# Splitting a weight panel in two counted halves on VectorE

## What is computed

```python
def reference(...):
    x = first_block(x, c, positions, g_mix, w_ada, b_ada, w_in, ..., g_final)
    return second_block(x, c_2, ctx_2, c_ctx_2, ada_w_2, ada_b_2, ..., ffn_w_out_2)

# first_block, each layer (shortened)
    u = rms_norm(x, g_mix[l]) * (1 + sc_a) + sh_a
    proj = u @ w_in[l]
    ...
    x = x + gt_a * (merged @ w_out[l])
    u = rms_norm(x, g_ffn[l]) * (1 + sc_f) + sh_f
    h = jax.nn.silu(u @ w_ffn_gate[l]) * (u @ w_ffn_up[l])
    x = x + gt_f * (h @ w_ffn_down[l])
```

## Time and profile before

| | us |
|---|---|
| median of 3 runs | 2088.14 |
| lowest, highest | 2082.11, 2090.48 |
| the profiled execution | 2090.16 |
| its span, first to last instruction | 2088.3 |
| TensorE: matmuls under way | 2017.8 |
| TensorE: loading weights | 1827.4 |
| VectorE busy | 1624.2 |
| ScalarE busy | 1170.3 |
| GpSimd busy | 148.0 |

### The profile page before, as it was taken

The page is one execution under the profiler, slowest core; times in us unless marked ns, Lnnn a source line. Parts: engine busy times, 40 slices in busy tenths (PEclk is TensorE's granted clock), DMA queues, the critical chain, the costliest instruction groups (busy, mean ns, idle before and its releaser), DMA issues.

```text
span 2088.3 us, 37048 instructions
## 1 busy us (share of the span) xinstructions
PE 2017.8 (97%) x13975; PEld 1827.4 (88%) x13975; DVE 1624.2 (78%) x2668; ACT 1170.3 (56%) x2116; POOL 148.0 (7%) x233
## 2 busy tenths in 40 slices
PE   6999999999999999998999999999999999999998
PEld 6988999999988999997876888888887888998997
DVE  7888879966688879978687889786979436657983
ACT  6757756645557756646636455352544226656862
POOL 0100000100000000004000300001102000000000
PEclk9999999999999999999999999999999999999999
DMA  9866548765766557866341234546634223244553
GB/s 363 284 204 210 180 173 273 274 223 170 241 217 207 184 170 265 302 237 213 119 164 55 101 131 157 196 140 234 219 133 142 91 92 100 91 152 136 196 184 110
DMA packets 106624, 383.03 MB, mean 183 GB/s; under 512 B 11504, under 2 KB 16128, under 8 KB 105184
## 3 DMA queue, kind: packets, MB, share of 16 engines
q1 hardware_dynamic: 77584, 280.21, 39.3%
q0 software_dynamic: 25792, 94.31, 13.6%
q10 hardware_dynamic: 3088, 6.29, 0.9%
HBM read 379.71 MB, written 1.05 MB: 182 GB/s over the span
## 4 chain that ended last, share of the span: by engine, by line
PE 74%; DVE 13%; issue 4%; ACT 4%; DMA 3%; POOL 0%; POOLq 0%; DVEq 0%; SPq 0%; ACTq 0%
PE ps L1104 18%; PE ps L1108 17%; PE ps L1107 17%; DVE ring_l L2394 3%; DVE ada_junk L2417 3%; PE ps L1125 3%; PE ps L1129 3%; PE ps L1130 3%; PE ps L1147 2%; DMA work<-adas_in 2%; PE ps L1150 2%; PE ps L1151 2%; ACT ring_r L1734 2%; PE ps L1684 1%; DMA ring<-tape_in 1%
## 5 line engine op out<-in xcount | busy, mean ns | idle before, releaser
L1104 PE MATMUL ps<-part,ring_l 128*128 128x256 f32 (+1 forms) x3373 | 1012.4, 300 | 8.3 <-DVE ring_l L2394 8.1
L1108 PE MATMUL ps<-part,ring_r 128*128 128x256 f32 (+1 forms) x3373 | 1005.4, 298 | 0.0
L1107 PE MATMUL ps<-part,ring_r 128*128 128x256 f32 (+1 forms) x3373 | 1004.6, 298 | 0.0
L2394 DVE TENSOR_TENSOR ring_l<-ring,ring_r 128x1024 fp32r<-128x1024 f32 x514 | 626.6, 1232 | 142.8 <-ACT ring_r L1734 140.5
L1734 ACT ACTIVATE ring_r<-ring 128x1024 fp32r<-128x1024 f32 x514 | 533.6, 1056 | 332.4 <-DMA ring<-tape_in 235.6
L1104 PEld LDWEIGHTS ps<-part,ring_l 128*128 128x128 f32 x3373 | 635.2, 188 | 40.5 <-issue 8.8
L1107 PEld LDWEIGHTS ps<-part,ring_r 128*128 128x128 f32 x3373 | 635.4, 188 | 25.3
L1108 PEld LDWEIGHTS ps<-part,ring_r 128*128 128x128 f32 x3373 | 634.6, 188 | 21.6
L2417 DVE SCALAR_TENSOR_TENSOR ada_junk<-work 128x1024 bf16<-128x1024 f32 x272 | 334.2, 1229 | 51.4 <-DMA work<-adas_in 39.7
L1147 PE MATMUL ps<-part,ring_l 128*128 128x256 f32 (+1 forms) x472 | 144.7, 307 | 20.1 <-DVE part L2394 10.6
L1150 PE MATMUL ps<-part,ring_r 128*128 128x256 f32 (+1 forms) x472 | 141.1, 299 | 0.0
(11 more groups left out here) (287 smaller groups left out, 2114.2 us busy)
## 6 DMA issues: line engine op xcount, KB each, us to landing
ring<-tape_in SPq DMA_DIRECT2D x514, 512.0 KB, 3.4
work<-adas_in POOLq DMA_DIRECT2D x176, 512.0 KB, 4.6
work<-ada_first_in SPq DMA_DIRECT2D x8, 1024.0 KB, 17.5
work<-bias_in ACTq DMA_DIRECT2D x1, 2048.0 KB, 7.9
x<-x_t_in SPq DMA_DIRECT2D x1, 1024.0 KB, 7.5
work<-cond_in POOLq DMA_DIRECT2D x1, 1024.0 KB, 8.7
x<-ctx_in ACTq DMA_DIRECT2D x1, 1024.0 KB, 9.3
x<-dist_in ACTq DMA_DIRECT2D x1, 1024.0 KB, 6.4
```

The source lines that it names most:

```text
L1104: mm = pe.matmul(dst, lhsT=wl, rhs=mr, start=(k == 0), stop=False)
L1107: pe.matmul(dst, lhsT=wr, rhs=mr, start=False, stop=False)
L1108: mm = pe.matmul(dst, lhsT=wr, rhs=ml, start=False, stop=(k == len(moving) - 1))
L2394: return dve.tensor_tensor(dst, whole, rounded_part.bitcast(F32), ALU.subtract)
```

## The change

A panel is split in two operations of four tiles (512 columns) each, and each counts `parted`, which so counts halves. TensorE waits at the first tile and at the fifth tile of a panel, for the count of the half that it then reads. The rounding on ScalarE stays one operation for a panel, and so do the load and the count of used panels.

```diff
 PANEL = TILES_PER_PANEL * TILE
+HALVES_OF_PANEL = 2
+HALF_PANEL = TILES_PER_PANEL // HALVES_OF_PANEL
...
                 slot = (base[0] + panel) % RING
-                if first == 0:
-                    pe.wait_ge(parted, base[0] + panel + 1)
+                if first % HALF_PANEL == 0:
+                    pe.wait_ge(parted, HALVES_OF_PANEL * (base[0] + panel) + first // HALF_PANEL + 1)
...
                     dve.wait_ge(rounded, q + 1)
-                    rest(ring_l[:, q % RING, :], ring[:, q % RING, :], ring_r[:, q % RING, :]).then_inc(parted, 1)
+                    for half in range(HALVES_OF_PANEL):
+                        cols = slice(half * HALF_PANEL * TILE, (half + 1) * HALF_PANEL * TILE)
+                        rest(ring_l[:, q % RING, cols], ring[:, q % RING, cols], ring_r[:, q % RING, cols]).then_inc(parted, 1)
```

## The result

The changed kernel takes 2095.5 us (median of 20 runs, 2089.2 to 2098.9), the kernel before beside it 2087.7 (20 runs, 2081.2 to 2094.0): a ratio of 1.0036, with a 95% interval of 1.0026 to 1.0046, or 7.5 us more. Forecast were 1.2 us more.

The account below looks back on a forecast made before the run. TensorE's own work was taken as the bound, with matmuls under way in 97% of the span. Costs of +3.9 less gains of 2.7 gave +1.2 us, from the median 2088.14 to 2089.3; range 2081 to 2098.

Parts of the forecast that it names:

- The price of a half: VectorE, every panel: two halves take 0.06 us more than a whole, 31 us in all; first half ready 0.53 earlier.
- Rival 3: Second half starts only after the first ends: 0.16 us a panel, 14.9 us over 93 splits, 2103.0; chance 0.09.
- Rival 4: TensorE's added waits are not free: at 0.02 us each 10.3 us, at 0.11 the time is 2145; chance 0.04.
- -0.9: First layer's projection down: two TensorE waits for splits give back 0.45 us each.
- The other gains: One wait each at the second block's first feed-forward, retention's gates and its output projection: -0.5 us each, -1.5 together.
- (a): The start, VectorE always busy: seven splits ahead of TensorE's last wait cost +0.4 us.
- (e): Attention starts and branch outputs of both layers, norm after the first projection down: some 16 splits, +0.9 us.
- (b): First layer's gate and up stage: VectorE's loop per pair of panels 6.00 instead of 5.88 us; +1.4 us.
- (c): Second layer's gate and up stage: 34 splits put VectorE 2.0 us behind; between 0 and 1.5, taken as 0.5.
- (d): Second block's convolutions, 1470 to 1526: 12 splits at 0.06 us, +0.7 us.
- -0.3: Second layer's projection down, four waits: 0.7 us cost for 12 splits against gains of 0.45 and 0.53.
- Rival 2: TensorE's step, 0.340 or 0.354 us a tile, changes in a gate and up stage: 2094.2 or 2084.4; chance 0.20.

Follow-up runs that it names:

- either of two edits: Against the changed kernel: panels 282, 285, 287 and 290 left whole, ratio 1.0014; or GpSimd's context runs put ahead of the DMA they followed, ratio 1.0010.

## Why the prediction was right or wrong

**The price of a half: right.** 1028 operations with a median of 0.684 us (forecast 0.69), two of them in 1.29 (forecast 1.29). In the first layer's gate stage the pair of panels, as in the earlier trace rows:

```profile
374.53 1.29 DVE L2396 TENSOR_TENSOR ring_l<-ring,ring_r 128x512 fp32r<-128x512 f32 x2
...
380.54 1.29 DVE L2396 TENSOR_TENSOR ring_l<-ring,ring_r 128x512 fp32r<-128x512 f32 x2
```

6.01 us, forecast 6.00. VectorE's busy time rose by 41.1 instead of 31; of that, the four caught halves take 12.3 more than four medians (6.49 + 3.08 + 3.06 + 2.38 - 4 x 0.69). Rival 3, a second half that starts only after the first has ended, falls with 1.29: the second starts 0.60 after the first, 0.09 before that one's end. The rule that the prediction set against its own price does not forbid this: the section of the Trainium skill that it names, "The DRAIN you can't avoid" in "VectorE: DVE Perf Modes", goes on that an operation that is not held starts earlier, and the trace agrees with that part.

**Rival 4: fell.** The steps across the middle of a panel are those inside it, 0.12 here, and the 45 panels from 1210 to 1470 cost 0.0 us in all. TensorE in the first layer's projection down, at the same first tile as the earlier trace rows, and at the fifth tile, where the new wait stands:

```profile
456.23 0.28 PE L1110 MATMUL ps<-part,ring_r 128*128 128x256 f32 x1
456.35 0.31 PE L1106 MATMUL ps<-part,ring_l 128*128 128x256 f32 x1
...
457.69 0.28 PE L1110 MATMUL ps<-part,ring_r 128*128 128x256 f32 x1
457.81 0.28 PE L1106 MATMUL ps<-part,ring_l 128*128 128x256 f32 x1
```

At the first tile 0.12 instead of 0.57: the wait is gone, 0.45 back, and the other one in that stage likewise. Forecast -0.9, by the table -0.8 (-1.5 less -0.6).

**The other gains: two were sized too small.** The second block's first feed-forward gave 0.5, as forecast. The output projection gave 1.9 and the gates 1.3, where 0.5 each was forecast. The waits became shorter by the forecast 0.53 (2.33 to 1.80, and 2.83 to 2.29). The rest is TensorE's clock, which the sum did not have. At the output projection it falls to 1.2 GHz for 3.4 us, after a wait of 2.3 us or more, in eight of the nine profiles in which TensorE waits there for a whole panel, and in none of the five with half waits. At the gates it is at 1.2 GHz for 3.4 us in four of these five, instead of 6.8 in all whole ones but one.

**The costs (a) to (e): of the right size one by one, too small in sum.** By the table (all halves less all whole): (a) with the start of layer 1's attention +0.8, (b) +0.9 instead of 1.4, (c) +0.9 instead of 0.5, (d) +1.5 instead of 0.7 with a wide spread, the second layer's attention +0.7. With layer 1's branches (145 to 343, not in the table), +0.7 with as wide a spread, and the scores of layer 1, +1.0, that is 6.5 where 3.9 were forecast. The scores cost what the sum did not have: in five of the six executions with halves in this stretch TensorE's granted clock falls to half there (1.2 GHz), in none of the eight others. Where it falls some 5 us earlier instead, as in four of the fourteen, the stretch costs 0.1 at most. The same 3 us in the changed kernel and before (the granted clock is the third number from the end):

```profile
139.50:142.50 3.00, 3.00 (x16) 3.00 (x15) 2.93 (x9) 2.64 (x10) 0.00 (x0) 0.50 0.02 5
```

```profile
139.50:142.50 3.00, 3.00 (x30) 2.63 (x28) 2.90 (x9) 2.81 (x11) 0.00 (x0) 1.00 0.00 0
```

Half as many matmuls in the same time. What sets it off was not tested; before it TensorE had stood 1.16 us (0.91 in the second profile) and 1.89 at two waits for VectorE, 0.49 and 1.65 in the kernel before.

**Where the mechanism failed: "-0.3" for the second layer's projection down.** The step reads: "I take 12 x 0.06 = 0.7 of cost, 0.45 for the first wait and 0.53 once for the others". It sized VectorE's queue by the durations of its operations and took the order on the other engines as unchanged: "No DMA, no queue and no operation of ScalarE is moved." GpSimd does not stand in that sentence, and it should have. Its runs begin a fixed time after the pair of products, 0.97 to 1.01 us into what VectorE does next (unless GpSimd is still at the run before), and two halves instead of a whole put another operation at that time. The trace of before showed both engines slowed by each other in just this stretch: splits of 1.5 to 1.76 us, operations of GpSimd of 1.7 instead of 0.74. I read the stretch by its windows and its chain. TensorE's two longest waits for splits there are, in the kernel before:

```profile
950.05 0.38 PE L1104 MATMUL ps<-part,ring_l 128*128 128x256 f32 x1 [1.73 <-DVE ring_l L2394]
957.40 0.39 PE L1104 MATMUL ps<-part,ring_l 128*128 128x256 f32 x1 [1.63 <-DVE ring_l L2394]
```

I took them as waits for a split and did not ask why splits there last longer than 1.22. The Trainium skill, "SBUF — State Buffer", section "SBUF: two separate sides", has the rule that would have sent me there: a VectorE operation with two SBUF inputs and a GpSimd operation that reads SBUF take a shared pair of ports as a lock, each for its whole instruction, and the other blocks. The alternating rows agree: the same 0.54 us is added to a whole (1.22 to 1.76) and to a half (0.69 to 1.23), less than the 0.70 of one operation of GpSimd. That VectorE waits for eight instructions and not for one is shown by the rows of this case alone.

Measured, the term is about +4.4 instead of -0.3, by the lined-up matmuls (2.7 of it standing, 1.7 TensorE's clock), and 4 to 5 us by the times (1.0034 and 1.0036 with the four second halves caught, 1.0014 and 1.0010 without, by either of two edits). The prediction named a stage that moves by more than about 2 us while its tiles keep their step as a sign that it is wrong; here the standing alone is more. Without that term the change costs 2 to 3 us, and the forecast of the rest was +1.5. That these come so near is in part luck: costs of 6.5 instead of 3.9 stand against gains of 4.5 instead of 2.4.

**Rival 2: the two steps are there, but in another stage, and not shown to follow from the change.** In the last feed-forward the first profile of the kernel before has the shorter step, that of the changed one the longer. The same 90 us in the two, TensorE busy for all of it at the full clock (PE's count is the first in brackets):

```profile
1910.00:2000.00 90.00, 90.00 (x796) 90.00 (x796) 86.54 (x152) 73.03 (x135) 0.00 (x0) 1.00 0.59 195
```

```profile
1910.00:2000.00 90.00, 90.00 (x767) 90.00 (x766) 85.85 (x179) 70.97 (x130) 0.00 (x0) 1.00 0.57 186
```

90 / 796 = 0.113 and 90 / 767 = 0.117 us a matmul, 0.340 and 0.352 a tile, 4.8 us over the stretch. The second profile of the kernel before has the longer step too, so its program does not fix it. All six executions with all panels in halves have the longer one, of the other eight four have it throughout. If the change favours it, that adds up to 2 us; if it is chance, it lies in the spread of the executions. This stays open. The step is not kept from one stall to the next, as the prediction has it: in the changed kernel it goes from 0.118 to 0.113 us a matmul near 874, in the second layer's gate stage, with no stall there.

**Why the range held: luck.** The sum was off by 6 us, and the range reached to 2098 for other reasons: rival 2, (c) at its upper end, and 3 us of spread. The mechanism that cost the time, GpSimd's runs, was in none of the rivals.

## What to carry to other kernels

Cutting an operation in two moves what comes at a fixed delay behind it: list the engines that start by a semaphore from the same queue, and see what their start now meets. An operation in the trace of before that lasts longer than its median (here 1.76 against 1.22) can be contention with another engine, as it was here; find the partner before its neighbours are changed. And a wait at half the work pays beyond the time by which the half is early: here about 4 of its 9 us came back in the stretch that GpSimd held up, and 2 at a wait that became only 0.53 shorter, where TensorE's clock then stayed up.

## What the hardware showed that I had not expected

- A subtraction of VectorE that a run of GpSimd's operations met 0.37 to 0.40 us after its start, and that followed directly on an operation of 512 columns, stayed until the whole run was over, in all twenty cases: 6.5 us (half) and 7.0 (whole) for eight operations, 3.1 and 3.6 for three, 2.4 and 2.9 for two. GpSimd ran at full pace meanwhile, 0.70 from start to start.
- A run that began at 0.17, or at 0.97 us or later, alternated with VectorE where VectorE had work, one operation each: a whole then took 1.76, a half 1.23, and GpSimd's operations 1.72 or 1.19. What makes the difference between the two is not settled; in this stretch starts between 0.18 and 0.37 and between 0.40 and 0.97 were not met.
- At the output projection TensorE's granted clock fell to 1.2 GHz after a wait of 2.3 us or more in eight of nine profiles, and after 1.80 us in none of five. That the half microsecond decides it was not tested.
- TensorE's step of 0.113 or 0.117 us a matmul at the same granted clock differs between two executions of the same program (1910 to 2000, first and second profile of the kernel before).
